# A norm weight vector brought to all partitions by TensorE instead of by a broadcast load, in an HGRN2 and pooling block on one Trainium2 core

## What is computed

```python
def rms_norm(x, w):
    xf = x.astype(jnp.float32)
    y = xf * lax.rsqrt(jnp.mean(xf * xf, axis=-1, keepdims=True) + EPS)
    return (y * w.astype(jnp.float32)).astype(x.dtype)
...
    z = jnp.concatenate([meta, x], axis=1)
...
        h = rms_norm(z, norm_w[l])
        p = (h @ w_in[l] + b_in[l]).astype(f32)
        q, fz, iv, g_hg, u, g_pool, m_hg, m_pool = jnp.split(p, split_at, axis=-1)
```

## Time and profile before

| what | value |
|---|---|
| median of 3 runs | 1064.03 us |
| lowest and highest run | 1062.83 and 1064.33 us |
| the profiled execution, its own time | 1062.84 us |
| its span in the profile | 1061.1 us |
| TensorE busy with matmuls, share of the span | 97% |
| VectorE, ScalarE, GpSimd busy | 74%, 46%, 9% |

### The profile page before, as it was taken

The page is one execution under the profiler, slowest core; times in us unless marked ns, Lnnn a source line. Parts: engine busy times, 40 slices in busy tenths (PEclk is TensorE's granted clock), DMA queues, the critical chain, the costliest instruction groups (busy, mean ns, idle before and its releaser), DMA issues.

```text
span 1061.1 us, 18864 instructions
## 1 busy us (share of the span) xinstructions
PE 1029.1 (97%) x7444; PEld 840.2 (79%) x7444; DVE 782.4 (74%) x1277; ACT 492.2 (46%) x833; POOL 96.5 (9%) x162
## 2 busy tenths in 40 slices
PE   7879999999999999999999999999999999999997
PEld 6658888888888888878888887788887787787886
DVE  7888787878787878787676777864569789979234
ACT  7663535454535454544443533444457246246222
POOL 2500010101010101010101010011100110000111
PEclk9999999999999999999999999999999999999999
DMA  6022020202020201122212122228323674455233
GB/s 262 1 80 80 22 81 21 81 21 81 21 78 24 67 35 63 39 81 71 98 42 90 60 90 80 70 76 295 121 104 99 230 286 150 167 182 178 79 107 128
DMA packets 36055, 104.61 MB, mean 99 GB/s; under 512 B 4576, under 2 KB 4576, under 8 KB 35968
## 3 DMA queue, kind: packets, MB, share of 16 engines
q1 hardware_dynamic: 22064, 65.61, 18.8%
q0 software_dynamic: 8240, 26.79, 6.8%
q10 hardware_dynamic: 5664, 11.02, 2.8%
HBM read 78.23 MB, written 25.17 MB: 97 GB/s over the span
## 4 chain that ended last, share of the span: by engine, by line
PE 82%; DVE 12%; issue 3%; ACT 1%; DMA 1%; POOL 0%; DVEq 0%; ACTq 0%; POOLq 0%
PE acc L1165 68%; PE levels L1302 2%; DVE w_lo L1531 1%; PE miscs L1324 1%; PE levels L1165 1%; DVE r_lo L2068 1%; PE miscs L1335 1%; PE miscs L1336 1%; PE acc L1206 1%; DMA gate_in<-smh_spill 1%; PE miscs L1165 1%; DVE att L1687 1%; PE acc L1350 1%; PE miscs L1279 1%; PE miscs L1342 1%
## 5 line engine op out<-in xcount | busy, mean ns | idle before, releaser
L1165 PE MATMUL acc<-r_hi,w_hi 128*128 128x512 f32 x1112 | 445.9, 401 | 15.1 <-DVE w_lo L1531 6.6
L1165 PE MATMUL acc<-r_hi,w_lo 128*128 128x512 f32 x1112 | 434.1, 390 | 0.0
L1165 PE MATMUL acc<-r_lo,w_hi 128*128 128x512 f32 x1112 | 433.9, 390 | 0.0
L1165 PEld LDWEIGHTS acc<-r_hi,w_hi 128*128 128x128 f32 x1112 | 208.8, 188 | 68.4 <-issue 20.0
L1165 PEld LDWEIGHTS acc<-r_hi,w_lo 128*128 128x128 f32 x1112 | 208.7, 188 | 45.2
L1165 PEld LDWEIGHTS acc<-r_lo,w_hi 128*128 128x128 f32 x1112 | 209.1, 188 | 39.8
L685 ACT ACTIVATE w_hi<-sum 128x512 fp32r<-128x512 f32 x156 | 97.8, 628 | 165.2 <-DVE sum L1567 82.8
L1531 DVE TENSOR_TENSOR w_lo<-sum,w_hi 128x512 fp32r<-128x512 f32 x156 | 106.3, 685 | 57.4 <-ACT w_hi L685 57.1
L1531 DVE TENSOR_TENSOR w_lo<-raw,w_hi 128x512 fp32r<-128x512 f32 x120 | 82.0, 686 | 63.9 <-ACT w_hi L685 63.8
L685 ACT ACTIVATE w_hi<-raw 128x512 fp32r<-128x512 f32 x120 | 74.5, 623 | 26.6 <-PE acc L1165 26.6
L1165 PE MATMUL acc<-wo_hi,m_hi 128*128 128x512 f32 x128 | 49.9, 390 | 0.6 <-DVE wo_lo L2204 0.6
(11 more groups left out here) (296 smaller groups left out, 1365.8 us busy)
## 6 DMA issues: line engine op xcount, KB each, us to landing
raw<-in_wstream SPq DMA_DIRECT2D x88, 512.0 KB, 3.6
xin<-in_x SPq DMA_DIRECT2D x8, 512.0 KB, 6.2
a_spill<-gt POOLq DMA_DIRECT2D x16, 256.0 KB, 3.6
c_spill<-pg POOLq DMA_DIRECT2D x16, 256.0 KB, 2.7
stage<-a_spill ACTq DMA_DIRECT2D x4, 1024.0 KB, 12.5
smh_spill<-zq POOLq DMA_DIRECT2D x16, 256.0 KB, 2.6
gate_in<-smh_spill SPq DMA_DIRECT2D x16, 256.0 KB, 5.1
part_spill<-zq POOLq DMA_DIRECT2D x16, 256.0 KB, 5.0
```

The lines of the kernel that those rows point to most:

```text
L1165: ins = pe.matmul(out_ap, a, b, start=first and n == 0, stop=final and n == 2, skip_group_check=partial)
```

## The change

The load of `nw` brings one row of 4 KB into partition 0 instead of 128 copies of it (512 KB). GpSimd writes 128 ones into a free piece of `hrow`, in partition 0. Two matmuls of 1 row by 128 by 512 columns, in float32 and with the row of ones as the stationary operand, put each half of `nw` into all 128 partitions of a PSUM bank (`acc[2]`, `acc[3]`). ScalarE copies the first half back to `nw`, between square_x(0) and square_x(1), and VectorE the second, between x_mean(0) and h_row(0). Then `h_row(0)` may run. The two matmuls stand first on TensorE, ahead of the first `keep_warm`.

```diff
@@ POOL
             steps.mark(pool.memset(ident[:, :], 0.0))
+            pool.memset(hrow[0:1, 1, 0:P], 1.0).then_inc(S["ones_made"], 1)
             steps.mark(pool.memset(minus_half[:, :], -0.5))
@@ ACT
-            act.dma_start(nw[:, :], norm_w[0:1, :].to_broadcast([P, D])).then_inc(S["norm_row_loaded"], 16)
+            act.dma_start(nw[0:1, :], norm_w[0:1, :]).then_inc(S["norm_row_loaded"], 16)
...
             square_x(0)
+            act.wait_ge(S["norm_spread"], 1)
+            act.activation(nw[:, 0:HALF], acc[2][:, :], ACT.Copy).then_inc(S["norm_copied"], 1)
             square_x(1)
@@ PE
+            pe.wait_ge(S["ones_made"], 1)
+            pe.wait_ge(S["norm_row_loaded"], 16)
+            for n in range(2):
+                ins = pe.matmul(acc[2 + n][:, :], hrow[0:1, 1, 0:P], nw[0:1, n * HALF:(n + 1) * HALF], start=True,
+                                stop=True)
+            ins.then_inc(S["norm_spread"], 1)
             pe.wait_ge(S["consts_made"], 1)
@@ DVE
             x_mean(0)
-            dve.wait_ge(S["norm_row_loaded"], 16)
+            dve.wait_ge(S["norm_spread"], 1)
+            dve.tensor_copy(nw[:, HALF:D], acc[3][:, :]).then_inc(S["norm_copied"], 1)
+            dve.wait_ge(S["norm_copied"], 2)
             h_row(0)
```

More of the change, by code:

```diff
@@ L162, in hybrid_block @@
         sem_names = [
-            "params_loaded", "logits_loaded", "norm_row_loaded", "x_loaded0", "x_loaded1", "x_loaded2", "x_loaded3",
+            "params_loaded", "logits_loaded", "norm_row_loaded", "ones_made", "norm_spread", "norm_copied", "x_loaded0", "x_loaded1", "x_loaded2", "x_loaded3",
             "x_loaded4", "early_loaded", "fifth_made",
```

## The result

The changed kernel takes 1066.62 us (median of 10 runs, 1064.91 to 1067.25) against 1064.07 us before (10 runs, 1062.83 to 1064.64): 2.5 us slower, a ratio of 1.0026 with a 95% interval of 1.0018 to 1.0034. The forecast was 1065.6 us in a range of 1064.0 to 1067.3. The time lies in the range and the direction is right, but the forecast said +1.6 us and within 0.2%, and it is 1.0 us more and 0.26%.

A forecast was written before the change was run, and what follows sets the result against it. TensorE bounds the kernel, VectorE's work the start before 24 us. Added products cost 1.8 us at the higher clock, less 0.2 slack: +1.6 on 1064.03 gives 1065.6 us, range 1064.0 to 1067.3.

The forecast's parts named there:

- What bounds the start: Before 24 us: VectorE's own work from 12.44 us on, plus whatever decides when its first subtraction can start.
- The load costs and gains nothing: At the start: 508 KB less traffic, x tile 1 up to 1.4 us sooner, costed at nothing.
- When the row lands: Landing of the 4 KB row of weights: taken as 3.0 us, between 2.4 and 3.8.
- The price of the products: Two one-row matmuls first on TensorE: four records of 0.85 us, 3.4 us in all, from 3.0 to 6.4.
- The moment of the rise: TensorE's clock rises at 7.46 us as before, so the added work costs 1.8 us at the higher rate.
- The rival: At TensorE's start: clock rises 4.4 us after keep_warm's first record, at 10.8 us; +3.2 us, 1067.2 us; chance 17%.
- the sum: TensorE's start to the end: +1.8 us at the transposes less 0.2 us of slack, +1.6 us, median 1065.6 us.
- A bound within it: At TensorE's start: the clock rival decides, passing 0.2% (2.1 us), once the rise comes later than about 9 us.
- The waits on VectorE and ScalarE: Copies of 0.60 and 0.68 us before `h_row(0)`: `h_row(1)` starts about 9.4 against 9.15 us, costing nothing.
- The chances: For the whole kernel: slower by over 0.2% 34%, within 0.2% 62%, faster 4%.
- The spread: For the whole time: the rise differs between executions, giving the forecast its own range of 1064.9 to 1066.4 us.

The follow-up runs named there:

- products of 128 rows: The changed kernel with its products spanning all 128 rows (ones in row 0 of a zero block, weight tile cleared first): 1067.43 us, ratio 1.0040.
- one row against 128: The kernel before plus two unread matmuls ahead of keep_warm: with one row 1067.25 us, ratio 1.0039; with 128 rows 1064.86 us, ratio 1.0017.
- the run with 128-row matmuls: The kernel before plus two unread matmuls of all 128 rows ahead of keep_warm: 1064.86 us, ratio 1.0017.
- the split load: The kernel before, broadcast load cut in two: rest behind x tile 1, 1063.00 us; behind x tile 2 without 4 keep_warm, 1063.14 us.

## Why the prediction came out as it did

- **What bounds the start: right.** VectorE is without a gap again from its first subtraction until the first real product (11.05 of 11.05 us from 14.95 to 26.00), and the shift of the first goes one for one into the second and to the end.
- **The load costs and gains nothing: right, to about a microsecond.** Two runs show it, without the load (ratio 0.9995) and with it cut in two (0.9997).
- **When the row lands: wrong, by 0.7 us, to the good side.** I took 3.0 between 2.4 and 3.8. It landed by 2.34, 1.5 us after its issue and just under my lower end; in three other profiles of the same load it was there by 2.35 to 2.61. The estimate by the Trainium skill (DMA: Bandwidth & Descriptors, Anatomy of one DMA), 2.8, is nearer, and still too late; the section gives its fit for loads that GpSimd issues, and ScalarE issues this one. I had priced a load with its queue neighbours in mind; with none ahead of it, it was faster, and with four x tiles ahead it took 4.35 us (products of 128 rows).
- **The price of the products: right, slightly short.** 3.7 us instead of 3.4. The four records start 0.98, 0.85 and 0.85 us apart, and keep_warm 0.99 us behind the last of them, where I had taken 0.85 for each.
- **The moment of the rise: the step that failed.** "If the clock rises at 7.46 as before" was the condition, and "all of the added work is in the end paid at the higher rate, 16 x 0.111 = 1.8 us" hung on it. The rise came at 10.0 us. With the row and the products as measured and the rise at 7.46, tile 0's transposes would have started at about 10.4 us (6 records of keep_warm until 7.46, then 26 x 0.111); they started at 11.66. So the 2.5 us by which the rise came later cost 1.2 us, which is more than the whole miss of 1.0 us. The row's early landing gave some back. The rival gave +3.2 with the row at 3.0, products of 3.4 us and the rise 4.4 us behind keep_warm's start. The row came 0.7 us earlier, the products took 0.3 us more, and the rise came 4.0 us behind keep_warm's start, worth 0.2 us: that is +2.6, and +2.5 was measured. The time lies in the range because the range reached to this rival's 1067.3, and not because the sum was right.
- **A bound within it: slightly off.** The rival was said to decide once the rise comes later than about 9 us. By the sum's own terms (0.213 against 0.111 us per record) the 2.1 us are passed at 8.5 us already.
- **The waits on VectorE and ScalarE: right.** The norm of tile 1 was even 0.3 us earlier than before, and TensorE came to it 3 us later.
- **The chances.** Slower by over 0.2% had 34%, about half of it from the rival that held, at 17%. That was too little. I had called it evidence against the rival that TensorE works without a gap, and the runs show that this is not what decides (one row against 128, both without a gap). The trace of before could not have told the two apart, since the only work ahead of its one rise was keep_warm.
- **The spread.** I had allowed the rise to move by some tenths of a microsecond. Behind keep_warm's start it was 4.0, 4.1, 4.9 and 6.2 us in the four profiles with one-row products ahead of 16 keep_warm, and 3.4 to 5.6 us in the five that start with keep_warm. Two microseconds of that are worth about one at tile 0's transposes, since a record takes half as long behind the rise. Runs of one kernel differ by 2 us and more (the changed one from 1064.91 to 1067.25), so the rise can explain a part of it.

What stays open: what matmuls of 2 to 127 rows ahead of keep_warm would do, since only 1 and 128 were run, what sets the moment within those 2 us, and why some executions have a stretch at the lower clock later on (below).

## What to carry to other kernels

Filler matmuls that raise TensorE's clock are real work for whatever stands behind them. Work put ahead of them is paid in full if it doesn't itself bring the rise, since the rise moves with the filler: the one-row matmuls moved keep_warm by 3.7 us and tile 0's transposes by 3.5. Work that brings the rise itself gets most of its price back: the full-row matmuls moved keep_warm by 3.5 us and the transposes by 1.3. Before a load is replaced by TensorE work, look at whether anyone waits for the load (here nobody did, 5.3 against 5.84 us) and at what stands behind TensorE's list at that moment. And when a sum rests on when the clock rises, ask what TensorE did before the rise in the trace, and whether the new work is of the same form.

## What the runs showed of the hardware that was not expected

- Two float32 matmuls of one row took as long as those of 128 rows (3.78 and 3.69 us), but the same 32 keep_warm records behind them took 5.80 instead of 3.73 us.
- A 4 KB row load, one packet in the trace, took 1.5 us when it was the first on ScalarE's queue, and 4.35 us when it was issued 1.2 us later among x tiles.
- With 8 instead of 16 keep_warm the kernel before got to the higher clock and lost it again: 0.50 granted from 10.2 to 13.4 us, after a stretch in which TensorE was busy 1.78 of 3.20 us. The changed kernel with 8 got there only at 14.1 us.
- Ten of the thirteen profiles have a stretch at the lower clock in the middle of the kernel too; their granted clock from 50 to 60 us is 0.83 to 0.87. In the run with 128-row matmuls (busy time by stretch, the granted clock behind POOL's column):

```profile
40.00:54.00 14.00, 9.88 (x43) 7.45 (x43) 11.49 (x17) 9.82 (x13) 3.79 (x10) 1.00 0.00 1
54.40:57.60 3.20, 3.20 (x9) 2.52 (x8) 3.20 (x6) 0.00 (x0) 0.00 (x0) 0.50 0.00 0
```

The profiles before, after and with one-row matmuls have none, although TensorE stands still there for the same 2.4 us (from 50.0 to 52.4 us in the profile before). This stretch costs nothing that lasts. By the chain of waits, before first and the run with 128-row matmuls second, that run is 1.1 us late ahead of it and 1.1 us late behind it:

```profile
47.11 2.94 PE acc L1165 x12
64.94 0.61 DVE fg L1631
```

```profile
48.21 2.90 PE acc L1165 x12
66.06 0.61 DVE fg L1634
```

The stretch near 24 us in the two runs with the split load did last, 1.6 us each.
- The column of the granted clock reads 1.00 in the first microseconds, where the spacing of the records says 1.2 GHz. At the start of a kernel the spacing is the better witness.
